# Selected, sliding and differential attention: query tiles walked from the last to the first

## What is computed

```
p = softmax(where(valid, q @ k.T * scale - slope * dist, -inf))
out[q_tile] = p @ v          # every tile of 128 queries stands for itself
```

## Time and profile before

| | us |
|---|---|
| median of three runs | 2819.24 |
| profiled execution | 2822.95 |
| its span | 2820.8 |
| stage "sl" (first score to last output) | 516.4 to 690.2 |
| stage "wi" | 690.5 to 815.8 |
| stage "hd" | 816.1 to 848.5 |
| stage "di" | 848.5 to 994.0 |

### The profile page before, as it was taken

How to read it: one execution, slowest core, us unless ns; L and a number is a source line. 1 busy time by engine, 2 the same in 40 slices (tenths; PEclk the granted TensorE clock), 3 DMA queues, 4 the chain that set the end, 5 groups by cost and what they waited for, 6 DMA issues and landing times. The chain is left out here.

```text
span 2820.8 us, 34813 instructions
## 1 busy us (share of the span) xinstructions
PE 2575.7 (91%) x12876; PEld 2119.4 (75%) x12876; DVE 1466.9 (52%) x3370; ACT 1013.2 (36%) x2275; POOL 180.5 (6%) x188
## 2 busy tenths in 40 slices
PE   8999986899996679997989999889799999999998
PEld 6887865777985668885658888666578887888877
DVE  5244266855888874218874732478672323223235
ACT  4223132444674442217861232344442223122132
POOL 2000000000000011101200001343000000000000
PEclk9999986799998989999999999899799999999999
DMA  4112120000000054110011132000541111111113
GB/s 149 31 46 78 56 62 1 1 1 1 1 1 1 1 175 116 38 27 14 25 53 49 49 131 101 30 1 1 194 157 38 49 55 47 49 49 46 49 55 143
DMA packets 105079, 153.05 MB, mean 54 GB/s; under 512 B 35408, under 2 KB 49872, under 8 KB 104912
## 3 DMA queue, kind: packets, MB, share of 16 engines
q1 hardware_dynamic: 96464, 125.67, 14.1%
q0 software_dynamic: 3840, 12.59, 1.1%
q10 hardware_dynamic: 4608, 12.58, 1.1%
HBM read 121.44 MB, written 29.36 MB: 53 GB/s over the span
## 5 line engine op out<-in xcount | busy, mean ns | idle before, releaser
L202 PE MATMUL banks<-mhT,mmwhi 128*128 128x512 f32 x1024 | 316.1, 390 | 3.9 <-ACT qsq L2925 2.8
L193 PE MATMUL banks<-mmwhi,fT 128*128 128x512 f32 x1024 | 315.6, 390 | 3.7 <-ACT qsq L2925 3.7
L193 PE MATMUL banks<-g1whi,hT 128*128 128x512 f32 (+1 forms) x1024 | 304.8, 381 | 7.9 <-ACT gates L428 2.9
L177 DVE TENSOR_TENSOR mmwlo<-mmwraw,mmwhi 128x512 fp32r<-128x512 f32 x144 | 97.1, 689 | 368.8 <-ACT mmwhi L172 368.8
L172 ACT ACTIVATE mmwhi<-mmwraw 128x512 fp32r<-128x512 f32 x144 | 89.3, 629 | 412.6 <-DMA mmwraw<-in_w_down 206.6
L193 PEld LDWEIGHTS banks<-mmwhi,fT 128*128 128x128 f32 x1024 | 191.8, 188 | 45.1 <-ACT qsq L2925 5.4
L202 PEld LDWEIGHTS banks<-mhT,mmwhi 128*128 128x128 f32 x1024 | 191.6, 188 | 45.4 <-ACT qsq L2925 4.1
L193 PEld LDWEIGHTS banks<-g1whi,hT 128*128 128x128 f32 x1024 | 188.7, 189 | 45.9 <-issue 4.4
L202 PE MATMUL banks<-mhT,mmwlo 128*128 128x512 f32 x512 | 199.3, 389 | 0.0
L193 PE MATMUL banks<-mmwlo,fT 128*128 128x512 f32 x512 | 199.3, 389 | 0.0
L193 PE MATMUL banks<-g1wlo,hT 128*128 128x512 f32 (+1 forms) x512 | 194.2, 379 | 0.0
(11 more groups left out here) (443 smaller groups left out, 5444.0 us busy)
## 6 DMA issues: line engine op xcount, KB each, us to landing
mmwraw<-in_w_up SPq DMA_DIRECT2D x64, 256.0 KB, 2.7
mmwraw<-in_w_down SPq DMA_DIRECT2D x64, 256.0 KB, 2.6
g1wraw<-in_w_in SPq DMA_DIRECT2D x56, 256.0 KB, 2.7
g3wraw<-in_w_in SPq DMA_DIRECT2D x40, 256.0 KB, 2.6
qx<-x_scratch SPq DMA_DIRECT2D x16, 512.0 KB, 6.8
xt<-in_x SPq DMA_DIRECT2D x8, 512.0 KB, 5.1
z_scratch<-zst POOLq DMA_DIRECT2D x16, 256.0 KB, 4.1
cw<-in_cmp_w SPq DMA_DIRECT2D x2, 2048.0 KB, 10.0
```

Source lines behind the costliest of these rows:

```text
L177: self.nc.vector.tensor_tensor(self.lo[n][:, c], self.raw[n][:, c], f32(self.hi[n][:, c]), ALU.subtract)\
L193: ins = self.nc.tensor.matmul(out, l, r[:, c], start=k == 0 and i == 0, stop=k == self.nk[j] - 1 and i == 2)
L202: ins = self.nc.tensor.matmul(out, l[:, col], r, start=k == 0 and i == 0, stop=k == self.nk[j] - 1 and i == 2)
```

## The change

Both loops that make the units count t from 7 down to 0. Heads keep their order inside a tile. Nothing else is edited: the same units with the same instructions are issued in another order, and the banks and turns are worked out for it.

```diff
     def nsa_units(kT, v, branch, k_first, table, sel):
         out = []
-        for t in range(NT):
+        for t in range(NT - 1, -1, -1):
             for h in range(NSA_HEADS):
...
     units = []
-    for t in range(NT):
+    for t in range(NT - 1, -1, -1):
         for h in range(DIFF_HEADS):
```

## The result

The changed kernel is slower: 2824.58 us median of 20 runs against 2819.41 of before, 5.2 us, with a ratio of 1.0023 (95% interval 1.0012 to 1.0034). Its runs reach from 2818.55 to 2846.44; those of before from 2816.97 to 2824.3. The profiled execution took 2823.53 us, with a span of 2821.4.

The account below looks back on a forecast made before the run. TensorE's work was taken to bound selected and sliding attention, a VectorE and ScalarE loop the differential stage. Terms +0.7 + 1.8 + 0.5 - 3.2 = -0.2 us, from the 2819.24 median to 2819.0; range 2813 to 2828.

Parts of the forecast that it names:

- Slow clock over t = 7 in "sl": Head of selected attention: dense t = 7 scores raise the clock after about 5 us, losing 1.9 us (bounds 0 and 9).
- the clock rival: Selected and sliding stages: clock rises no sooner under t = 7 than under small tiles, +12.6 us, 2831.8 us; chance 0.14.
- Slow clock saved on t = 0 and 1: Selected attention: small tiles no longer meet the slow clock at the head, saving 2.7 us (bounds 0 and 9).
- Ends and t = 0 of "sl": Selected attention: idle at start and end adds 1.1 us; the clock falling again over t = 0 adds 0.4.
- "wi": Sliding attention: -2.5 saved, +2.8 slow head, +0.4 clock fall over t = 0, +1.1 ends; +1.8 us.
- "hd": Stretch between sliding and differential attention: follows slow units, so another slow-clock stretch, +0.5 us (bounds 0 and 1.7).
- "di": Differential attention: start +3.6, between first and last L1269 -1.8, end -5.9, slow clock +0.9; -3.2 us.
- The 0.9 us set aside for it: Differential attention: loss taken for the clock falling in the first t = 7 turns, at most 5.1 us per whole unit.
- the rival built on it: Differential attention: a whole t = 7 unit at half clock makes TensorE late, 5.1 instead of 0.9, 2823.2 us; chance 0.12.
- The rule on transposes: Early t = 7 turns: by the skill, transposes do not engage full clock; the prediction followed the profile row against it.

Follow-up runs that it names:

- e4: Full change plus 12 unread TensorE products at the end of compressed attention, against the kernel before: median 2.6 us faster, ratio 0.9982 to 1.0.
- e2: Only sliding and differential attention reversed, selected attention in first order, against the kernel before: median 4.6 us faster, ratio 0.9974 to 0.9993.
- e17: Full change plus block-selection product in float32r, zero-padded from 16 to 128 rows, against the kernel before: 17.2 us faster, ratio 0.9923 to 0.9952.
- e5: First order kept, 12 unread TensorE products added at the end of compressed attention, against the kernel before: 0.7 us faster, ratio 0.9982 to 0.9999.
- e3: Only differential attention reversed, against the kernel before: median 5.8 us faster, ratio 0.9969 to 0.9992.
- e18: Selection product in float32r zero-padded to 128 rows, only differential attention reversed, against the kernel before: 19.3 us faster, ratio 0.9916 to 0.9941.
- e10: The changed kernel run again unaltered, against the kernel before: median 3.3 us slower, ratio 0.9999 to 1.0023.
- e13: Full change with the 16-row selection product in float32r instead of bfloat16, against the kernel before: median 26.5 us slower, ratio 1.0036 to 1.0089.
- e15: First order kept, 16-row selection product in float32r instead of bfloat16, against the kernel before: 8.3 us slower, ratio 1.0016 to 1.0033.

## Why the prediction was wrong

The forecast was 2819.0, no change; measured are 2824.58 and a change beyond its interval. The time lies in the range; that it would rise was given 0.17. Step by step:

- **Slow clock over t = 7 in "sl": the step that failed.** Forecast: some 5 us at half, 1.9 us lost. Measured: 18.6, 11.9 and 25.3 us at half in three traces, and 8.1, 5.1 and 11.1 us lost against the warm start (31.4 us from first score to t = 6). It is the clock rival, to which I gave 0.14, near its full price of 9 us in "sl" and absent in "wi". What I weighed against it, "products of 512 columns", did not look at their rows: every third of them has 16 [the third line in each group of the second listing above]. The row that should have warned stood in the argument, TensorE busy for 17.52 of 18.00 us at half clock.
- **Slow clock saved on t = 0 and 1.** Forecast 2.7 us. At full clock t = 1 took 11.35 us between its first L1254 and that of t = 0, not the 10.0 taken, against 12.2 before: 0.8 saved instead of 2.2. Why the small tiles gain so little is not shown; waits for the other engines would do it.
- **Ends and t = 0 of "sl".** e4 has all but the failed term: -2.0 us, where the terms -2.7, +0.4 and +1.1 gave -1.2. That the sum is close is partly luck: t = 1 saved 0.8 where 2.2 was forecast, so all else comes to about -1.2 by difference, where its terms made +1.0.
- **"wi": +0.8, forecast +1.8.** 5.7 us at half clock as said (6), and started at full clock (e2) it takes 125.3: the slow head costs 0.8, not 2.8. By the same run the rest of the reversed order is worth -0.1, not the forecast -1.0. The units have no selection product.
- **"hd": +0.1, forecast +0.5.** It began with 5.8 us of half clock, and TensorE waited for VectorE's L752 in it anyway, 4.2 us in 13 waits.
- **"di": -3.8, forecast -3.2; right by its steps.** The rows of after, for the start, a turn of t = 7, and the end:
```profile
857.32 0.47 PE L1180 MATMUL banks<-dkT,dqT 128*128 128x512 f32 x1 [1.05 <-PEq L716]
...
862.57 0.16 DVE L1269 RECIPROCAL dist<-dist 128x1 f32<-128x1 f32 x1 [1.31 <-ACT dix L1230]
...
863.35 1.28 DVE L1275 SCALAR_TENSOR_TENSOR dix<-dix,dist,dix 128x1024 f32<-128x1024 f32 x1
...
869.39 1.28 DVE L1275 SCALAR_TENSOR_TENSOR dix<-dix,dist,dix 128x1024 f32<-128x1024 f32 x1
...
875.50 1.29 DVE L1275 SCALAR_TENSOR_TENSOR dix<-dix,dist,dix 128x1024 f32<-128x1024 f32 x1
...
995.70 0.16 DVE L1269 RECIPROCAL dist<-dist 128x1 f32<-128x1 f32 x1 [0.30 <-ACT dix L1230]
...
998.64 0.35 DVE L1292 TENSOR_SCALAR o_diff<-banks,dist 128x128 f32<-128x128 f32 x1 [0.46 <-PE banks L1206]
```
  First score to first L1269 is 5.25 us (forecast 5.5), a turn 6.11 (869.39 to 875.50) against 6.10 in the earlier trace rows, last L1269 to the end 3.3 (2.9). The clock did fall for 3.4 us, from 864.3, and it cost nothing: the turn in which it fell took 6.04 us (863.35 to 869.39), and TensorE still waited for L1275 once per unit:
```profile
PE banks L1194 <- DVE dix L1275: 43.9, 32, 2.2
```
  The 0.9 us set aside for it, and the rival built on it, were not needed.
- **The rule on transposes.** The rule of the Trainium skill (TensorE: Matmul & The Clock Gate, Part 4: PE-mode transpose) stands against the earlier trace rows, with 18 transposes at half clock and full clock after, and the traces since agree with the rows: in "hd" of the changed kernel the clock rose at 830.3, after nothing but transposes. The rule pointed to the right outcome for the wrong reason: the first transpose of the changed "sl" stands at 528.25, and by then the clock had been low for 10.1 us over score products alone, where the same products with 128 rows brought it up in 5.0 (e17).

Why some executions keep the clock low much longer than others is not settled; no trace was taken of one of the changed kernel above 2830 us. Nor is the 16-row product all there is to it: before, the clock stayed low for 18.0 us over t = 0 and 1, which have none. There too products stood far apart for their columns, 0.21 us for 128 columns, where 512 took 0.43 in e17, but no run tests whether that held the clock.

## What to carry to other kernels

Before tiles are put in another order, mark in the trace where the clock is low, and ask which products will stand there afterwards: here about 18 us of half clock cost 8 us under full tiles, and 1 or 2 under tiles short of work (an estimate: 0.8 on t = 1, and 0.6 from first score to t = 1, 8.5 us before against 7.9 in e5). Put what is bound by another engine, or has products of all 128 rows, in front. Try padding a product of few rows that stands among products of many: here 16 rows made into 128 took 16.4 us off "sl" in the first order (173.5 in e3, 157.1 in e18), four times the 3.8 that the best order took off "di".

## What the runs showed of the hardware

- At half clock, a stream that the profile shows as busy all the time need not bring the full clock: 25.3 us busy of 25.3 at 0.51 in e10, and 230.4 of 230.4 at 0.50 in one of the long executions of e13, with one score product in three of 16 rows; with 128 rows in the same place it rose after 5.0 us (e17). The 16 rows also put the products 0.56 us apart instead of 0.43 at half clock, and which of the two matters is open.
- Once the clock was up, the same 16-row products did not bring it down: in "sl" before, 1.00 over all tiles t = 4 to 7, and in e15 too, with the float32r product that in e13 left the clock low.
- A product of 16 rows between products of 128 rows slows its neighbours at full clock as well: starts 0.32 us apart with 16 rows of bfloat16, 0.23 with 128 rows of float32r, for 512 columns each. The rows do it, not the type: in e15, with 16 rows of float32r, the products of a set start 0.31 to 0.43 us apart, and "sl" was 6.3 us longer than with bfloat16.
